# A two-layer mixer and FFN block on one core: the last product of each half layer in two token parts

## The reference, cut to what matters

```python
u = modulate(rms_norm(x, g_pre_mix[l]), sh1, sc1) @ w_in[l]
...
mix = jnp.concatenate([merge(o_a), o_b, merge(o_c), o_d], axis=-1) @ w_out[l]
x = x + gt1 * rms_norm(mix, g_post_mix[l])
ffn = swiglu(modulate(rms_norm(x, g_pre_ffn[l]), sh2, sc2), w_ffn_in[l], w_ffn_out[l])
x = x + gt2 * rms_norm(ffn, g_post_ffn[l])
```

## Time and profile before

| | us |
|---|---|
| median of 3 runs (1972.38 to 1974.13) | 1973.86 |
| the profiled execution, its own time | 1975.02 |
| its span, first to last instruction | 1973.2 |
| TensorE busy, of the span | 1730.3 (88%) |
| VectorE, ScalarE, GpSimd busy | 984.6, 623.0, 146.6 |
| mean granted TensorE clock | 0.94 |

### The profile page before, as it was taken

One profiled execution on the slowest core, in us unless ns is written; L12 is line 12 of the kernel. 1 busy time (PEld: TensorE's weight loads), 2 busy tenths in 40 slices (PEclk: granted clock), 3 DMA queues, 4 the chain that ended last, 5 costly groups with the idle time before them and its releaser, 6 DMA issues.

```text
span 1973.2 us, 24651 instructions
## 1 busy us (share of the span) xinstructions
PE 1730.3 (88%) x10460; PEld 1525.4 (77%) x10460; DVE 984.6 (50%) x1606; ACT 623.0 (32%) x817; POOL 146.6 (7%) x184
## 2 busy tenths in 40 slices
PE   2799987857969999999999969998847899999996
PEld 1799955656959999999999959975535577887874
DVE  7844447782775554554622371116693343133334
ACT  3322235743252222221122152234543443232231
POOL 1000000000500000000000400001000300000003
PEclk9899998868989999999999989999858999999998
DMA  8443331001313333442422212242100223332332
GB/s 314 136 128 128 128 59 48 2 2 43 129 38 125 126 128 128 128 128 96 129 65 64 75 72 75 75 103 40 40 1 22 64 75 96 96 97 85 97 96 96
DMA packets 80238, 176.61 MB, mean 90 GB/s; under 512 B 38896, under 2 KB 39408, under 8 KB 79872
## 3 DMA queue, kind: packets, MB, share of 16 engines
q1 hardware_dynamic: 67008, 123.62, 20.5%
q0 software_dynamic: 13120, 51.41, 7.5%
HBM read 172.91 MB, written 2.10 MB: 89 GB/s over the span
## 4 chain that ended last, share of the span: by engine, by line
PE 78%; DVE 14%; ACT 4%; issue 2%; DMA 2%; DVEq 0%; ACTq 0%; SPq 0%
PE psum L692 69%; PE psum L798 2%; PE psum L754 2%; DVE s_sb L1147 1%; PE psum L809 1%; DMA ada_0a<-in_adaT 1%; DVE f_t L1101 1%; PE psum L832 1%; DVE hk L1269 1%; DVE x L1105 1%; DVE hd L1283 1%; DVE tmp L1079 1%; PE psum L722 1%; DVE psum L1345 1%; PE psum L949 1%
## 5 line engine op out<-in xcount | busy, mean ns | idle before, releaser
L692 PE MATMUL psum<-h_hi,w_hi 128*128 128x384 f32 (+1 forms) x1872 | 549.5, 353 | 56.5 <-DVE h_lo L1086 31.4
L692 PE MATMUL psum<-h_lo,w_hi 128*128 128x384 f32 (+1 forms) x1872 | 547.1, 352 | 0.0
L692 PE MATMUL psum<-h_hi,w_lo 128*128 128x384 f32 (+1 forms) x1872 | 546.4, 351 | 0.0
L1008 DVE TENSOR_TENSOR w_lo<-raw,w_hi 128x1024 fp32r<-128x1024 f32 x194 | 240.6, 1241 | 465.0 <-ACT w_hi L496 464.7
L692 PEld LDWEIGHTS psum<-h_hi,w_hi 128*128 128x128 f32 x1872 | 345.3, 190 | 81.0 <-issue 57.3
L496 ACT ACTIVATE w_hi<-raw 128x1024 fp32r<-128x1024 f32 x194 | 205.7, 1060 | 566.9 <-DMA raw<-in_wstream 566.9
L692 PEld LDWEIGHTS psum<-h_lo,w_hi 128*128 128x128 f32 x1872 | 346.3, 190 | 19.3
L692 PEld LDWEIGHTS psum<-h_hi,w_lo 128*128 128x128 f32 x1872 | 345.2, 190 | 19.9
L1019 DVE CUSTOM_DVE_ANT_0 psum<-ada_w,c_b 128x1024 f32<-128x1024 f32 x160 | 206.4, 1290 | 8.5 <-DVE ada_t L1019 0.2
L1047 DVE TENSOR_TENSOR tmp<-tmp,psum 128x768 f32<-128x768 f32 (+1 forms) x44 | 36.1, 821 | 279.9 <-PE psum L692 279.9
L692 PE MATMUL psum<-hid_hi,w_hi 128*128 128x384 f32 (+1 forms) x528 | 161.0, 359 | 15.4 <-DVE w_lo L1008 13.3
(11 more groups left out here) (168 smaller groups left out, 1525.4 us busy)
## 6 DMA issues: line engine op xcount, KB each, us to landing
raw<-in_wstream SPq DMA_DIRECT2D x196, 512.0 KB, 3.5
ada_w<-in_adaT POOLq DMA_DIRECT2D x80, 512.0 KB, 4.2
ada_0a<-in_adaT SPq DMA_DIRECT2D x6, 1024.0 KB, 14.4
fn_l<-in_dftL POOLq DMA_DIRECT2D x2, 2048.0 KB, 8.1
na_r<-in_rpb SPq DMA_DIRECT2D x64, 64.0 KB, 3.2
x<-in_xT POOLq DMA_DIRECT2D x2, 1536.0 KB, 14.2
ada_0b<-in_adaT SPq DMA_DIRECT2D x2, 1024.0 KB, 19.1
out_xT<-x SPq DMA_DIRECT2D x4, 512.0 KB, 2.8
```

What stands on the lines that cost most here:

```text
L692: mm = pe.matmul(ps[u][:, at:at + hi - lo], w[:, slot, k], r[:, k, lo:hi], start=first, stop=last)
L1008: dve.tensor_tensor(w_lo[:, k % RING].rearrange("p c n -> p (c n)"), raw[:, k % RING], w_hi[:, k % RING].rearrange("p c n -> p (c n)").bit ...
```

## The change

The eight products of `wout` and of the last `out` piece become sixteen, eight over the first part of the tokens and eight over the second: 512 and 256 columns where there are 768 tokens, 256 and 256 where there are 512 (`PARTED`). The second part goes over the blocks in the order 5, 6, 7, 0, 1, 2, 3, 4: the last three tiles are still in the ring, the other five are loaded a second time (`KEPT`; `load_of` says which load a product uses). The first pair of such a phase is interleaved over the first part.

The norms are done by parts. Post-norm of part 0 stands in VectorE's program between the products of part 1, two chunks after each of four products (`norm_chunks`; one or two after each of six in the FFN's last phase), each multiply now waiting for its end before the add; ScalarE squares x of part 0 in the same stretch, now into six buffers `xsq` of their own, and TensorE sums after products `m1` and `m2` of part 1. Then come pre-norm of part 0, post-norm of part 1, its squares, root and pre-norm. The next phase's interleaved pair runs over part 0, then over part 1 (`after_norm`), with two tiles side by side; its banks hold the parts at columns 0 to 511 and 512 to 767. The pre-norm at the start is in two parts too. GpSimd's squares run by parts, and x is stored in eight DMAs instead of four. Lines of bookkeeping that only rename counters are left out below.

```diff
+PARTED = tuple((b, 0) for b in range(N_OUT)) + tuple((b, 1) for b in (5, 6, 7, 0, 1, 2, 3, 4))
+KEPT = 5
...
+            PRODUCT0[layer, name], LOAD0[layer, name] = product, len(LOAD_TILE)
+            for j, (b, part) in enumerate(PARTED if name in ("wout", LAST_OUT) else [(b, 0) for b in range(n)]):
+                if part and b >= KEPT:
+                    FREE_AFTER[LOAD0[layer, name] + b] = product + 1
+                else:
+                    LOAD_TILE.append(tile + b)
+                    FIRST_USE.append(product)
+                    FREE_AFTER.append(product + 1)
+                product += 1
+            tile += n
...
+def parts(T):
+    return ((0, LAT, 0), (LAT, TOK, 1)) if T == TOK else ((0, LAT // 2, 0), (LAT // 2, LAT, 0))
...
+def norm_products(kc):
+    return (4, 5) if kc == NC else (6, 7)
+def norm_chunks(kc, m):
+    return {1: (0, 1), 2: (2, 3), 3: (4, 5), 4: (6, 7)}.get(m, ()) if kc == NC else \
+        {1: (0,), 2: (1,), 3: (2, 3), 4: (4,), 5: (5, 6), 6: (7,)}.get(m, ())
...
+            def stream(r0, r1):
+                for r in range(r0, r1):
+                    sp.wait_ge(blk_done, FREE_AFTER[r - RING])
+                    sp.dma_start(raw[:, r % RING], wstream[LOAD_TILE[r]]).then_inc(raw_ld[r % RING], 16)
...
+            for part, (lo, hi, _) in enumerate(parts(LAT)):
+                for c in range(0, NC, 2):
+                    sp.wait_ge(x_upd, (4 * DEPTH - 2 + part) * NC + c + 2)
+                    sp.dma_start(outT[:, c:c + 2, lo:hi], x[:, c:c + 2, lo:hi]).then_inc(s_out, 16)
+            sp.wait_ge(s_out, 16 * NC)
...
+            def parted_phase(l, name, kc, copy):
+                T, norm = width[l], 2 * l + (name != "wout")
+                final = norm == 2 * DEPTH - 1
+                m1, m2 = norm_products(kc)
+                for j, (b, part) in enumerate(PARTED):
+                    q = PRODUCT0[l, name] + j
+                    lo, hi, _ = parts(T)[part]
+                    splits(q)
+                    if copy:
+                        act.wait_ge(blk_done, q + 1)
+                        act.activation(f_t[:, b, lo:hi], ps[q % 2][:, 0:hi - lo], ACT.Copy).then_inc(bank_free[q % 2], 1)
+                    m = j - N_OUT
+                    if m == -1:
+                        last_square(l, name, 0)
+                    if m == 0:
+                        inverse_root(T, 0)
+                    if not final:
+                        if m == m1 - 1:
+                            x_squares(norm, T, 0, 0, 4)
+                        if m == m2 - 1:
+                            x_squares(norm, T, 0, 4, 4)
+                        if m == m2:
+                            inverse_root(T, 0)
+                last_square(l, name, 1)
+                if not final:
+                    round_hi(T, 0, 0, 4)
+                inverse_root(T, 1)
+                if not final:
+                    round_hi(T, 0, 4, 4)
+                    x_squares(norm, T, 1, 0, NC)
+                    inverse_root(T, 1)
+                    round_hi(T, 1, 0, NC)
...
+                            if nsq[0] >= 2:
+                                act.wait_ge(sq_used, nsq[0] - 1)
+                            act.activation(sq[:, c % 2, lo:hi], x[:, c, lo:hi], ACT.Square).then_inc(sq_ready, 1)
+                            nsq[0] += 1
+                        inverse_root(TOK, part)
+                        round_hi(TOK, part, 0, NC)
                     act.wait_ge(consts_done, 2)
                     act.activation(lbt[:], lbt[:], ACT.Exp).then_inc(consts_done, 1)
...
+            def parted_phase(l, name, rhs_hi, rhs_lo, kc, ready):
+                T = width[l]
+                m1, m2 = norm_products(kc)
+                first_pair(l, name, rhs_hi, rhs_lo, kc, tuple((lo, hi, 0) for lo, hi, _ in parts(T)[:1]), ready)
+                for j in range(2, len(PARTED)):
+                    lo, hi, _ = parts(T)[PARTED[j][1]]
+                    product(l, name, j, rhs_hi, rhs_lo, kc, ((lo, hi, 0),))
+                    m = j - N_OUT
+                    if m == 0:
+                        late_mean_square(T, 0)
+                    if (l, name) != (DEPTH - 1, LAST_OUT):
+                        if m == m1:
+                            mean_square(T, 0, x_square, 0, 4)
+                        if m == m2:
+                            mean_square(T, 0, x_square, 4, 4)
+                if (l, name) == (DEPTH - 1, LAST_OUT):
+                    late_mean_square(T, 1)
+            def after_norm(l, name, T):
+                first_pair(l, name, h_hi, h_lo, NC, part_pieces(T, 0), chunks_split(), False, lambda: late_mean_square(T, 1))
+                mean_square(T, 1, x_square, 0, NC)
+                first_pair(l, name, h_hi, h_lo, NC, part_pieces(T, 1), chunks_split())
...
-                mean_square(TOK)
-                ready = chunks_split(2)
+                    for part in range(2):
+                        mean_square(TOK, part, lambda c, lo, hi: sq[:, c % 2, lo:hi], 0, NC)
+                        first_pair(l, "proj", h_hi, h_lo, NC, part_pieces(TOK, part), chunks_split(), part == 1)
...
+            def post_norm(T, part, chunks):
+                lo, hi, v = parts(T)[part]
+                for c in chunks:
+                    dve.scalar_tensor_tensor(f_t[:, c, lo:hi], f_t[:, c, lo:hi], col_gg[:, c, v:v + 1],
+                                             rstd[:, lo:hi], ALU.mult, ALU.mult).then_inc(pn_m, 1)
+                    nm[0] += 1
+                    dve.wait_ge(pn_m, nm[0])
+                    dve.tensor_tensor(x[:, c, lo:hi], x[:, c, lo:hi], f_t[:, c, lo:hi], ALU.add).then_inc(x_upd, 1)
+                    nx[0] += 1
...
+            def parted_phase(l, name, kc, add, ada=None):
+                T = width[l]
+                final = (l, name) == (DEPTH - 1, LAST_OUT)
+                for j, (b, part) in enumerate(PARTED):
+                    q = PRODUCT0[l, name] + j
+                    lo, hi, _ = parts(T)[part]
+                    splits(q)
+                    if add:
+                        dve.wait_ge(blk_done, q + 1)
+                        dve.tensor_tensor(f_t[:, b, lo:hi], f_t[:, b, lo:hi], ps[q % 2][:, 0:hi - lo], ALU.add)\
+                           .then_inc(bank_free[q % 2], 1)
+                    if ada and part == 0 and j % 2:
+                        ada_pair(j // 2 + ada[0], ada[1], j // 2 + ada[2])
+                    m = j - N_OUT
+                    if m == 0:
+                        if name == "wout":
+                            if l == 0:
+                                dve.wait_ge(ada_copied, 17)
+                            post_columns(l, GT1, G_POST_MIX)
+                            pre_columns(l, SH2, SC2, G_PRE_FFN)
+                        else:
+                            post_columns(l, GT2, G_POST_FFN)
+                            if not final:
+                                dve.wait_ge(ada_copied, 41)
+                                pre_columns(l + 1, SH1, SC1, G_PRE_MIX)
+                        root_ready()
+                    if m >= 0:
+                        post_norm(T, 0, norm_chunks(kc, m))
                 dve.wait_ge(x_upd, nx[0])
+                if not final:
+                    pre_norm(T, 0)
+                root_ready()
+                post_norm(T, 1, range(NC))
+                dve.wait_ge(x_upd, nx[0])
+                if not final:
+                    pre_norm(T, 1)
```

More of the change, by code:

```diff
@@ new lines, with lay_out_products @@
+KEPT = 5
+PRODUCT0, LOAD0 = {}, {}
+LOAD_TILE, FIRST_USE, FREE_AFTER = [], [], []
+def lay_out_products():
+    product = tile = 0
+    for layer in range(DEPTH):
+        phases = [("proj", N_PROJ), ("wout", N_OUT)]
+        for p, kc in enumerate(FFN_CHUNKS):
+            phases += [(("in", p), 2 * kc), (("out", p), N_OUT)]
+        for name, n in phases:
+            PRODUCT0[layer, name], LOAD0[layer, name] = product, len(LOAD_TILE)
[8 more added lines that the diff above has]
+            tile += n
@@ new lines, with load_of, loads_due, part_pieces @@
+lay_out_products()
+def load_of(layer, name, j):
+    if name in ("wout", LAST_OUT):
+        b, part = PARTED[j]
+        return LOAD0[layer, name] + (N_OUT + b if part and b < KEPT else b)
+    return LOAD0[layer, name] + j
+def loads_due(product):
+    return [r for r in range(len(FIRST_USE)) if FIRST_USE[r] == product + 2]
+def parts(T):
+    return ((0, LAT, 0), (LAT, TOK, 1)) if T == TOK else ((0, LAT // 2, 0), (LAT // 2, LAT, 0))
+def part_pieces(T, part):
+    lo, hi, _ = parts(T)[part]
+    return ((lo, hi, lo),)
@@ L87, in backwards, with as_product @@
+def as_product(row, T, by_part=False):
+    return row.rearrange("p (b t) -> p b t", b=2) if T == TOK and not by_part else row
 def backwards(ap):
@@ L285, in hybrid_kernel @@
         block = ctx.enter_context(nc.Block())
-        TP = [tile_counts(l) for l in range(DEPTH)]
         full = [l < DEPTH - 1 for l in range(DEPTH)]
@@ L684, in _ @@
         @block.tensor
         def _(pe):
```

(38 more changed lines are left out.)

399 lines of the change are left out of this document (181 added, 218 removed).

## The result

The change makes the kernel slower: 2028.6 us (median of 4 runs, 2027.8 to 2033.1) against 1974.0 beside it, ratio 1.0283, 95% interval 1.0265 to 1.0301. That is +54.6 us where +29.9 was forecast, and above the range's upper end of 2014. The direction and most of the places were right; the size was not.

What follows compares the result with a forecast made beforehand. The prediction took TensorE's queue to bound the kernel (78% of the chain), with VectorE holding it at the start. Its terms, 10.2 - 0.8 + 3.5 + 9.4 + 7.6 = +29.9 us, gave 2003.5 us, range 1988 to 2014.

Steps and rivals of the forecast that it cites:

- A: Start, up to the first phase's third product: +10.2 us, bounds 8 and 12, with VectorE as the chain.
- B: Layer-0 output product and its tail: -0.8 us, from phase +10.0 and tail -10.8.
- C: Last FFN product of layer 0 and its tail: +3.5 us, from phase +11.5 and tail -8.0.
- D: Layer-1 output product and its tail: +9.4 us, from phase +10.4 and tail 35.1 against 36.0.
- E: Last phase of layer 1, to the last x: +7.6 us, 58.3 against 50.7.
- The ones-matmuls: Sums over part 0 in TensorE's queue between part 1's products: 8.8 + 8.8 + 4.6 + 0.9 = 23 us.
- The ring: Three weight slots, about 6.1 us from product end to product start: waits 2.7 (C), 3.1 (D), 10.9 us (E).
- rival 2: Weight tiles landing in 4.5 us under denser loads, on twenty more tiles: +11 us, about 2014; chance 0.12.
- The tails: From a parted phase's last product to the next phase's third product: 39.1 (B), 41.9 (C), 35.1 us (D).
- Rival 1: Faster: part 1's products cover all of part 0's norm in the four phases, 38.7 us less, 1965; chance 0.07.
- Rival 5: Clock falls in narrow phases, 256-column product matmuls in layer 1 slower: some +50 us, 2055; chance 0.02.

Runs made afterwards that it cites:

- e8_squares_reload: Changed kernel with GpSimd squaring only the first block of each part and part 1's tiles of blocks 0 to 4 not loaded or split again: ratio 1.0102.

## Why the prediction fell short, step by step

- **A** was right in kind and 2.5 us low (12.7 for 10.2, its bound 12): the pair over part 0 ended at 71.7, not 69.8, and the third product followed the rest as worked out. Undoing the order alone gives it back.
- **B, C, D, the phases: the step that failed.** The prediction wrote "Waits add 1.2: VectorE must fit two chunks of post-norm (2.8 us) and a w_lo (1.15) into each 2.9 us product", and in C and D it counted 2.7 and 3.1 us of ring waits and nothing for VectorE: 7.0 us in all for what isn't TensorE's own work. With the squares and the reloads both gone (e8_squares_reload) the three phases take 79.1, 59.0 and 57.0 us instead of 84.7, 67.8 and 60.6, some 18 us less, so that is what these waits cost. Two things were mispriced. First, VectorE's durations were taken from stretches where GpSimd is idle, while in the parted phases GpSimd squares beside it: the phases B, C, D grew by 15.5, 15.7, 14.3 us for 10.0, 11.5, 10.4, and by 10.7, 12.1, 11.8 without the squares. Second, a reloaded tile costs VectorE a w_lo in a queue that already holds an add or nothing and the norm for every narrow product; the prediction let it cost only where the ring was late. The contention could have been read in the trace of before, where a w_lo of 1.22 us alone lasts 2.05 (VectorE, then GpSimd at the same time):

```profile
1937.12 2.05 DVE L1008 TENSOR_TENSOR w_lo<-raw,w_hi 128x1024 fp32r<-128x1024 f32 x1 [1.82 <-ACT w_hi L496]
```

```profile
1937.06 1.04 POOL L421 TENSOR_TENSOR sq<-f_t 128x512 f32<-128x512 f32 x1
1938.17 2.15 POOL L423 TENSOR_TENSOR sq<-sq 128x512 f32<-128x512 f32 x1
```

- **The ones-matmuls** were charged to TensorE as 23 us in line. Leaving most of them out gave nothing, because in the changed kernel they lie beside VectorE's work, which lasts longer. Where VectorE has room (e8_squares_reload) the phases are still 9.9, 6.9 and 10.7 us longer than before, near the price of the sums and, in D, the narrow matmuls (8.8, 8.8 and 7.3). So the size was not far off, but it doesn't come on top of VectorE's time (read from these two runs, not tested by itself). That the growth without the squares comes within 1.4 us of the forecast is therefore partly luck.
- **The ring** (rival 2, landings of 4.5 us) is not the cause: the median landing is 3.6 us, and taking 20 landings away gives 2.6 us by the times and nothing by the stages. In the last phase three of them stand in the chain, and the way from slot to product took 6.9 us (1976.93 to 1983.84) where 6.1 was priced.
- **The tails**: 40.1 us after B (39.1 forecast), 43.6 after C (41.9), 35.9 after D (35.1). Right within 1.7, save that the tail before C was 51.2 us where the sum used 49.9, which made the forecast of C 1.3 us too high by its own terms. The idle time in the middle of each part-0 pre-norm, forecast at 3.0, is 3.5, 4.5 and 3.7.
- **E**: 61.9 for 58.3. It doesn't move with the squares (0.2 us), hardly with the w_lo alone (1.4) and not with the landing alone, but by 5.0 us when both go: either of the two keeps it late. Undoing the phase gives 10.1 us by its trace, 9.7 by the times.
- **Rival 1** (faster, if the phases grow by under 13.5 us together): B, C and D alone grew by 45.5. **Rival 5** (the clock falls in narrow phases) didn't come: 256-column matmuls start every 0.12 us, as forecast, save behind waits.

In sum 24.7 us were missed by the times, 22.1 by the stages. Of the 22.1 the squares are 10.9 (B, C and D's phases), A is 2.5, E 3.6, the rest of the three phases 2.7 and the tails some 2. How the 8 us come about that go only with ScalarE's w_hi stays open: no run takes the w_hi away alone.

## What to carry to other kernels

Price an engine's work with rows from a stretch in which its neighbours do what they will do beside it afterwards; a duration from a quiet stretch is a lower bound. When a product is cut into narrow ones, list for every engine what it does per product, not per column: here the second weight split and the norm stayed or came anew while TensorE's share shrank to 2.2 us. And when parts are to overlap, check that the first part's squares and root don't queue the second part's behind them, which alone cost 10.7 us at the start.

## What the runs showed of the hardware

- VectorE instructions with two SBUF inputs lasted up to twice as long while GpSimd read SBUF (256-column multiply up to 0.96 us for 0.48, 512-column one 1.22 for 0.75, w_lo 2.06 for 1.22), and GpSimd's 256-column square 0.89 on average in C's phase for 0.61 alone. The w_lo at 1154.07 got 0.54 us longer with a GpSimd sum beside it for 0.68 us, so VectorE didn't stand still for all of that time. Adds from PSUM and VectorE beside GpSimd memsets were at full pace.
- Taking ones-matmuls out from between products went with a fall of TensorE's granted clock from 1.00 to 0.66 in the next stretch, after waits of 1.5 and 2.5 us, so part of the work that was left out came back as slower matmuls (one place; over the program 0.930 to 0.933 for 0.937 to 0.940).
